# One core, a layer with a 64-expert mixture: the first expert block's transposes and gate/up products put ahead of the shared expert's third down product

## What is computed

```
h = modulate(rms_norm(x))                       # 640 tokens x 1024
idx, w = route(h)                               # 8 of 64 experts for each token
routed: for each block of rows of one expert:   # w_gate, w_up 1024x256, w_down 256x1024
    hb = silu(xb @ w_gate[e]) * (xb @ w_up[e]);  rows = hb @ w_down[e]
shared = (silu(h @ ws_gate) * (h @ ws_up)) @ ws_down
x + gate * (routed + shared), then a last rms_norm
```

## Time and profile before

| what | value |
|---|---|
| time, median of 3 executions | 1043.44 us (1042.91 to 1045.49) |
| the profiled execution's own time | 1045.96 us |
| its span in the profile | 1044.1 us |
| TensorE busy over the span | 1005.5 us (96%) |
| bytes moved by DMA | 321.64 MB, mean 308 GB/s |
| HBM read and written | 316 GB/s over the span |

### The profile page before, as it was taken

One profiled execution on the slowest core, in us unless ns is written; L12 is line 12 of the kernel. 1 busy time (PEld: TensorE's weight loads), 2 busy tenths in 40 slices (PEclk: granted clock), 3 DMA queues, 4 the chain that ended last, 5 costly groups with the idle time before them and its releaser, 6 DMA issues.

```text
span 1044.1 us, 17787 instructions
## 1 busy us (share of the span) xinstructions
PE 1005.5 (96%) x7124; PEld 454.2 (44%) x7124; DVE 333.2 (32%) x839; ACT 227.0 (22%) x537; POOL 161.5 (15%) x233
## 2 busy tenths in 40 slices
PE   6999999999999999999999999999999999989996
PEld 3655556565455553444333333343333333423342
DVE  0122225865126772322111111121111111212388
ACT  1211104666122340112111111121111111212111
POOL 1000010300132022111221112112221121111000
PEclk9999999999999999999999999999999999989998
DMA  9965407500101199999999999999999999997896
GB/s 375 405 252 192 161 32 192 231 2 2 60 21 41 48 381 393 388 410 423 421 420 419 419 420 417 413 420 414 416 412 413 410 402 390 422 370 301 347 409 258
DMA packets 59676, 321.64 MB, mean 308 GB/s; under 512 B 9748, under 2 KB 10396, under 8 KB 31560
## 3 DMA queue, kind: packets, MB, share of 16 engines
q1 hardware_dynamic: 43184, 272.71, 65.0%
q0 software_dynamic: 14240, 43.34, 10.6%
q10 hardware_dynamic: 2168, 4.43, 1.1%
HBM read 298.78 MB, written 31.39 MB: 316 GB/s over the span
## 4 chain that ended last, share of the span: by engine, by line
PE 80%; DMA 11%; DVE 5%; ACT 2%; issue 1%; SPq 1%; POOLq 0%; DVEq 0%; ACTq 0%
PE bank L2120 27%; PE bank L2140 13%; PE bank L1711 8%; DMA ring<-in_w_up 7%; PE bank L1882 7%; PE bank L2092 4%; PE bank L1976 3%; PE bank L1738 2%; PE bank L1909 2%; PE bank L1700 2%; PE bank L1989 2%; DMA ring<-expert_rows 2%; PE bank L1895 2%; PE bank L1982 1%; PE bank L1866 1%
## 5 line engine op out<-in xcount | busy, mean ns | idle before, releaser
L2120 PE MATMUL bank<-ring,reg_h 128*32 128x512 f32 x2448 | 334.2, 595 | 6.3 <-DMA ring<-in_w_up 4.6
L2120 PEld LDWEIGHTS bank<-ring,reg_h 128*32 128x32 f32 x2448 | 99.3, 110 | 190.8 <-issue 190.7
L2140 PE MATMUL bank<-ring,reg_y 128*32 128x512 f32 x1224 | 170.5, 594 | 2.8 <-ACT reg_y L1075 2.0
L2120 PE MATMUL bank<-reg_p,reg_h 128*32 128x512 f32 x688 | 143.8, 602 | 0.5 <-DMA ring<-in_w_up 0.5
L1538 DVE TENSOR_TENSOR reg_h<-reg_p,bank 128x256 f32<-128x256 f32 x49 | 20.6, 421 | 320.8 <-ACT reg_p L1093 280.0
L1093 ACT ACTIVATE reg_p<-bank 128x256 f32<-128x256 f32 x49 | 18.8, 383 | 310.8 <-PE bank L2120 310.8
L1711 PE MATMUL bank<-ring,reg_h 128*128 128x384 f32 (+2 forms) x256 | 84.3, 487 | 0.0
L769 POOL DMA_INDIRECT expert_rows<-reg_y,rowc x47 | 47.2, 1004 | 239.6 <-DVE reg_y L1523 229.3
L2140 PEld LDWEIGHTS bank<-ring,reg_y 128*32 128x32 f32 x1224 | 46.5, 110 | 83.7 <-issue 79.1
L1523 DVE TENSOR_SCALAR reg_y<-bank,reg_p 128x512 f32<-128x512 f32 x49 | 36.8, 750 | 129.4 <-PE bank L2140 129.2
L2140 PE MATMUL bank<-reg_p,reg_y 128*32 128x512 f32 x344 | 72.3, 593 | 0.0
(11 more groups left out here) (279 smaller groups left out, 968.4 us busy)
## 6 DMA issues: line engine op xcount, KB each, us to landing
ring<-in_w_gate SPq DMA_DIRECT2D x51, 1024.0 KB, 13.7
ring<-in_w_up SPq DMA_DIRECT2D x51, 1024.0 KB, 22.2
ring<-in_w_down SPq DMA_DIRECT2D x51, 1024.0 KB, 20.3
ring<-in_w_mod SPq DMA_DIRECT2D x21, 1024.0 KB, 7.3
ring<-expert_rows SPq DMA_DIRECT2D x19, 1024.0 KB, 14.5
reg_p<-in_w_gate SPq DMA_DIRECT2D x13, 1024.0 KB, 12.8
reg_p<-in_w_up SPq DMA_DIRECT2D x13, 1024.0 KB, 20.5
reg_p<-in_w_down SPq DMA_DIRECT2D x13, 1024.0 KB, 23.7
```

Source lines behind the costliest of these rows:

```text
L2120: last = pe.matmul(bank[2 + p][R * j:R * j + R, :], xg_t[:, p, k * P + R * j:k * P + R * j + R], w_gu(homes[n % SLOTS])[:, k], start=(k == ...
L2140: last = pe.matmul(bank[y_banks(b)[hf]][R * j:R * j + R, :], h_t[:, p, i * P + R * j:i * P + R * j + R], w_dn(homes[n % SLOTS])[:, i, 512 ...
```

## The change

In TensorE's list, `shared_down(2)` moves from ahead of block 0's transposes to behind block 0's gate/up products, and `shared_h_t(4)` from ahead of block 0's gate/up products to behind block 1's transposes. No instruction is added or taken away, and no other engine's list is changed.

```diff
@@ TensorE, between shared_h_t(3) and block_gate_up(1) @@
             pe.wait_ge(s_tab, 1)
             pe.wait_ge(s_trip, 1)
             pe.wait_ge(s_shm, 1)
-            shared_down(2)
             block_transposes(0, 0, 16)
             groups = pe.value_load(trip[0:1, 0:1], min_val=0, max_val=XGROUPS)
-            shared_h_t(4)
             pe.sem_inc(s_epe, 1)
             pe.wait_ge(s_shm, 2)
             block_gate_up(0)
+            shared_down(2)
             block_transposes(1, 1, 16)
+            shared_h_t(4)
             shared_down(3)
             block_gate_up(1)
             shared_down(4)
```

## The result

| | before | changed |
|---|---|---|
| median of 22 executions each | 1046.01 us | 1050.76 us |
| lowest to highest | 1042.91 to 1050.25 | 1046.03 to 1052.60 |
| ratio | | 1.0043, 95% interval 1.0033 to 1.0053 |
| profiled execution: time, span | 1045.96, 1044.1 us | 1049.39, 1047.6 us |

The changed kernel is slower by 0.43%, 4.5 us.

The account below looks back on a forecast made before the run. TensorE and DMA were taken as both full from 440 to 920 us, weights late at the end; TensorE 3.1 us late, weights 2.0 late, so 1043.44 + 2.0 = 1045.4 us, +0.19%, range 1042.6 to 1048.6.

Parts of the forecast that it names:

- The step that failed: Block 0's gate/up products start at 398.4, 0.8 us earlier than before, and end at 405.4.
- a rival of 0.30: Clock falls to 0.50 in the new gap, block 0's products 3.0 us longer; +4.2 to +5.0 us in all; chance 0.30.
- The gap before block 0's transposes: From 393.31 to about 396.3 TensorE only waits for gather 0: 3.0 us of idle time.
- `shared_down(3)` behind VectorE's product: Before block 1's products, VectorE's product is ready at 410.25, TensorE at 410.4: the cover just does, no wait.
- The loads behind block 1 at 421.0: Loads after block 1's products come 3.1 us later but still find a queue at 421.0: no cost, or tenths.
- The weights 2.0 us late (0 to 3.1): Weights arrive between 0 and 3.1 us late, taken as 2.0; the wait at 927.7 ends at 931.7 + 2.0.
- The gain of 0.8 us: Loads that wait for block 0's gate/up products, issued at 406.41 before, come 0.8 us earlier, gaining up to 0.8 us.
- the down loads of experts 5 and 6: Issued at 431.5 instead of 428.45, 3.1 us later; the loss is +0.6 us at best, +3.1 at worst.
- Nothing is added later, nothing caught up: What the weights lose before about 440 us stays, and nothing is added after, as there is backlog later.
- The 5.2 us of waits: TensorE's three waits for up weights after 385 us, the longest 4.0 us; it can be 5.2 us late at no cost.
- The backlog rival: Late down loads still land in their old time and TensorE's 3.1 us vanish in its waits: 0, 1043.4; chance 0.13.
- the faster rival: Wait at 927.7 shrinks from 4.0 to 2.0 us, the clock stays, 3.0 us of slow products go: 1040.0; chance 0.07.

Follow-up runs that it names:

- `shared_down(2)` alone: Against the kernel before, only shared_down(2) moved behind block 0's gate/up products, shared_h_t(4) staying ahead of them; ratio 1.0056 (1.0035 to 1.0076).
- the two filled kernels: The changed kernel with throwaway shared_down(2) products, 3.44 us, ahead of block 0's transposes, run on two chips; ratios 1.0030 and 1.0022 against the kernel before.
- early dose: The kernel before with one throwaway copy of shared_down(3)'s products ahead of the real ones, 3.44 us; ratio 1.0027 (1.0015 to 1.0038).
- the second filled kernel: The changed kernel with 4 throwaway calls (8 products, 3.44 us) ahead of block 0's transposes; ratio 1.0022 (1.0007 to 1.0036) against the kernel before.
- The early doses: The kernel before with one and with two throwaway copies of shared_down(3)'s products, 3.44 and 6.9 us; ratios 1.0027 and 1.0056.
- the dose at block 10: The kernel before with block 10's down products done twice, and three times; ratios 0.9988 (0.9973 to 1.0004) and 1.0016 (1.0000 to 1.0032).
- the first filled kernel: The changed kernel with a throwaway copy of shared_down(2)'s 8 products in its old place; ratio 1.0030 (1.0016 to 1.0043) against the kernel before.

## Why the prediction was wrong, point by point

The step that failed is the one in which block 0's gate/up products run at the full clock and end at 405.4: the fall of the clock stood in a rival of 0.30 and with nothing in the sum, and it came in every profile with the gap. With the clock kept at its full level by throwaway products the kernel lost 2.3 and 3.1 us (0.7 to 3.8 and 1.7 to 4.5 by their intervals), against 2.0 forecast; with the fall it cost 4.5. A smaller part failed too, the loads behind block 1, which were put at nothing. The range ended at +0.49% of the median of 1043.44 us, so it held the ratio; it did not hold the median measured, of which 2.6 us are the higher median of the kernel before.

- **The gap before block 0's transposes: right.** Forecast 3.0 us, released by the gather; measured 3.6 in the profile, and 3.0 to 3.8 in the five profiles that have the gap.
- **The clock: the step that failed.** I gave 0.30 to a fall in the gap. It fell in four profiles of four, and in that of `shared_down(2)` alone. I had compared the new idle time, 3.0 us, with 4.0 (fell) and 1.7 (stayed) and called it nearer to the one that did, and then still gave it less than one half. The idle time behind the transposes, which the rival counted in, isn't needed for the fall: in three of the five profiles the clock fell before it. Alone, in the two filled kernels, its 0.9 us left the clock at 1.00. The price was stated as 3.0 us; measured 1.4 to 2.8. The rival's result, +4.2 to +5.0 us, is what was measured, but partly by luck: its price of 3.0 us lies above what the profiles show, and its base of 2.0 us below the 2.3 and 3.1 of the filled kernels.
- **`shared_down(3)` behind VectorE's product: the cover did not do.** The step said "ready at 410.25", just under TensorE's 410.4. It took the product of `shared_down(2)` as ended after 3.44 us, the distance at which the next matmul may follow; as seen from the reader of the bank it takes 3.64 or 3.65. In the same way the transposes end for their reader after 1.14 to 1.18 us and not 0.9. The wait is 0.4 us (L1505). So even with the gap filled and the clock at full level, block 1's products start at 414.36 and 414.83, counted from a `shared_h_t(3)` that ends 0.3 us earlier and 0.1 later than before: 3.9 to 4.0 us late where the step gave 3.1.
- **The loads behind block 1 at 421.0: a term put at nothing.** The step said "No cost, or tenths", since a load issued at 408.44 would land at 422.1. That landing was read from the kernel before, where the loads of 417.94 and 418.37 were under way beside it. It doesn't say how long the engines would have work without them. In the early dose, where the next loads come 3.4 us later, the four loads' 4.2 MB were through about 14.5 us behind their first issue (421.3 us), against 15.7 for the landing at 422.1. So the engines ran dry before the next loads came: in the changed kernel those were issued at 423.32, in a hole. Gather 3 and the two zero scatters had moved back too (gather 3 by 6.1 us, to 415.44), but the hole is there in the early dose as well, where they did not move (0.87 above). From 415 to 425 us the second filled kernel, with the clock at full level, shows:

```profile
415.00:425.00 10.00, 10.00 (x70) 3.49 (x63) 2.85 (x4) 0.38 (x1) 2.93 (x5) 1.00 0.77 286
```

  against 1.02 in the kernel before. That is 2.5 us of DMA time; in the early dose it is 1.5.
- **The weights 2.0 us late (0 to 3.1): mis-sized.** The last wait for weights ended at 931.70 before and at 936.72 after, 5.0 us later in the profiles, of which the products behind it gave 1.2 back (8.77 us against 9.98); the chain of the changed kernel there:

```profile
910.70 25.88 DMA ring<-in_w_up
...
936.72 8.77 PE bank L2120 x64
```

  The gain of 0.8 us that I set against the loss did not come: block 0's products ended at 407.33 and not at 405.4, and in the second filled kernel, with the clock at full level, at 405.58, 0.3 us better than before when its earlier start is taken off. For the down loads of experts 5 and 6 the sum had a loss of 0.6 to 3.1 us; the share from 428 to 440 us gives 1.2.
- **"Nothing is added later, nothing caught up": right.** The early doses pass on 0.8 to 0.9 of each microsecond, the dose at block 10 nothing that can be told of the first 3.4. The 5.2 us of waits are real slack, but only for lateness that arises once loads queue up; early lateness makes the weights late by the same amount.
- **The backlog rival and the faster rival: wrong**, both for want of a backlog before 440 us. Their mechanism exists, at block 10.
- The Trainium skill's rule to issue a DMA early, compute and wait late (DMA: Bandwidth & Descriptors, Rules for kernel authors) gave +3.4 us with the length of `shared_down(2)`: nearer to the measured 4.5 than my sum, though it has no term for the clock, and without the clock's fall 2.3 and 3.1 were measured. The reading of its other rule (Perfetto Trace Analysis, Identifying the Most-Contended Engine), by which TensorE's idle time would cost nothing, does not hold in this stretch: the DMA engines' work is set off by TensorE's progress. At block 10, where 3.43 us of added TensorE time cost nothing that can be told, the runs agree with it.

Open: how the 4.5 us divide between the clock and the rest. On one chip the clock has 3.9 points of a thousand of 6.1; by the first filled kernel it has 1.3 of 4.3, with overlapping intervals. The size of the fall differs from execution to execution, and the four profiles say 1.4 to 2.8 us. Open too: how much of the gap has to be filled to keep the clock.

## What to carry to other kernels

When work is moved out of a wait for a DMA, put the fall of the clock into the sum and not beside it: here 3.0 to 3.8 us of idle time cost the clock in five profiles of five, and 3.44 us of throwaway products in its place kept it in two of two. Before a filler is built, see in the profile how long one call of it takes. Where two resources are both full, ask at each place whether there is a queue in front of the second: lateness of the first is free, up to the waits it can use up, where a load takes 18 to 29 us to land behind others, and costs nearly its whole length where loads land in 5 to 14 and the DMA engines run dry between them. And when reading such a queue from the trace of before, take out of it the transfers that the change itself delays.

## What the runs showed of the hardware

- The granted clock fell from 1.00 (2.4 GHz) to 0.50 (1.2 GHz) in every profile with the gap, between the start of block 0's transposes and that of its products. Its price differed: those products took 8.4 us twice and 9.7 to 9.8 us twice in the changed kernel and 9.0 in `shared_down(2)` alone, for 7.00 at the full level.
- A stretch of throwaway products made a kernel faster than the same kernel without them: 1.0022 (1.0007 to 1.0036) against 1.0061 (1.0046 to 1.0076), same chip, 3.44 us of added work in what had been idle time.
- The clock's fall at 928 us of the kernel before, worth 3.0 us there, was gone in the profile of the kernel in which TensorE was made later, by 6.9 us at block 10.
